# One level of Strassen's scheme for the gate and up products of a two-layer hybrid block, on one core of a Trainium2 chip

## The reference

```
def swiglu(x, w_gate, w_up, w_down):
    return (jax.nn.silu(x @ w_gate) * (x @ w_up)) @ w_down
x = x + 0.5 * swiglu(rms_norm(x, norm), w_gate, w_up, w_down)   # D_MODEL = 1024, D_FF = 2816
```

## Time and profile before

| | us |
|---|---|
| three runs, median (lowest to highest) | 1998.88 (1998.53 to 1999.64) |
| span of the profiled execution, first to last instruction | 1996.9 |
| TensorE busy | 1968.5 |
| VectorE busy | 1076.8 |
| ScalarE busy | 771.1 |
| GpSimd busy | 50.0 |

### The profile page before, as it was taken

How to read it: one execution, slowest core, us unless ns; L and a number is a source line. 1 busy time by engine, 2 the same in 40 slices (tenths; PEclk the granted TensorE clock), 3 DMA queues, 4 the chain that set the end, 5 groups by cost and what they waited for, 6 DMA issues and landing times.

```text
span 1996.9 us, 25404 instructions
## 1 busy us (share of the span) xinstructions
PE 1968.5 (99%) x9054; PEld 1613.8 (81%) x9054; DVE 1076.8 (54%) x1673; ACT 771.1 (39%) x1110; POOL 50.0 (3%) x86
## 2 busy tenths in 40 slices
PE   7999999999999999999999999999999999999999
PEld 5888888888778888888888888877778778888887
DVE  5444444767674444446544444456989854444444
ACT  4222222477773222224332222354555852223222
POOL 1000000000000000000000000011111000000000
PEclk9999999999999999999999999999999999999999
DMA  4254433321122222233322233267765352332223
GB/s 166 101 122 121 137 96 100 110 74 64 55 84 95 95 95 96 99 100 105 106 95 95 95 96 102 96 163 168 158 153 133 87 137 96 97 103 95 95 95 105
DMA packets 60863, 213.80 MB, mean 107 GB/s; under 512 B 6616, under 2 KB 6872, under 8 KB 60792
## 3 DMA queue, kind: packets, MB, share of 16 engines
q1 hardware_dynamic: 52080, 184.97, 28.2%
q0 software_dynamic: 6192, 22.55, 6.2%
q10 hardware_dynamic: 2520, 5.36, 1.5%
HBM read 185.32 MB, written 4.72 MB: 95 GB/s over the span
## 4 chain that ended last, share of the span: by engine, by line
PE 89%; DVE 6%; ACT 3%; issue 2%; DMA 0%; SPq 0%; DVEq 0%; ACTq 0%
PE ps_unit L546 28%; PE ps_unit L548 28%; PE ps_unit L547 28%; DVE cv L1795 1%; DVE isc L1776 1%; PE ps_t L675 1%; DVE top L1774 1%; PE ps_s L546 1%; PE ps_y L547 0%; PE ps_y L548 0%; ACT w_hi L947 0%; PE ps_y L546 0%; PE ps_misc L636 0%; ACT L962 0%; DVE pt_lo L1543 0%
## 5 line engine op out<-in xcount | busy, mean ns | idle before, releaser
L947 ACT ACTIVATE w_hi<-raw 128x1024 fp32r<-128x1024 f32 x301 | 319.2, 1061 | 1019.9 <-PE ps_unit L548 1009.8
L546 PE MATMUL ps_unit<-xs_hi,w_hi 128*128 128x512 f32 x1768 | 697.3, 394 | 11.9 <-DVE xs_lo L1358 11.1
L547 PE MATMUL ps_unit<-xs_lo,w_hi 128*128 128x512 f32 x1768 | 688.9, 390 | 0.0
L548 PE MATMUL ps_unit<-xs_hi,w_lo 128*128 128x512 f32 x1696 | 660.9, 390 | 0.0
L1350 DVE TENSOR_TENSOR w_lo<-raw,w_hi 128x1024 fp32r<-128x1024 f32 x301 | 368.1, 1223 | 84.4 <-ACT w_hi L947 84.3
L546 PEld LDWEIGHTS ps_unit<-xs_hi,w_hi 128*128 128x128 f32 x1768 | 332.3, 188 | 87.8 <-DVE w_lo L1350 9.3
L547 PEld LDWEIGHTS ps_unit<-xs_lo,w_hi 128*128 128x128 f32 x1768 | 332.6, 188 | 68.5 <-issue 1.7
L548 PEld LDWEIGHTS ps_unit<-xs_hi,w_lo 128*128 128x128 f32 x1696 | 318.8, 188 | 66.9
L546 PE MATMUL ps_unit<-a_hi,w_hi 128*128 128x512 f32 x892 | 350.4, 393 | 2.4 <-DVE t L1472 0.8
L547 PE MATMUL ps_unit<-a_lo,w_hi 128*128 128x512 f32 x892 | 347.5, 390 | 0.0
L548 PE MATMUL ps_unit<-a_hi,w_lo 128*128 128x512 f32 x845 | 329.2, 390 | 0.0
(11 more groups left out here) (236 smaller groups left out, 1292.6 us busy)
## 6 DMA issues: line engine op xcount, KB each, us to landing
raw<-w_stream_dram SPq DMA_DIRECT2D x344, 512.0 KB, 3.5
w_lo<-raw POOLq DMA_DIRECT2D x28, 512.0 KB, 5.2
w_lo_3rd<-raw POOLq DMA_DIRECT2D x15, 512.0 KB, 5.3
skew<-table ACTq DMA_DIRECT2D x1, 2560.0 KB
bias_t<-skew ACTq DMA_DIRECT2D x1, 2048.0 KB, 9.7
out_dram<-xt SPq DMA_DIRECT2D x8, 256.0 KB, 2.0
xt<-xt_in_dram SPq DMA_DIRECT2D x7, 256.0 KB, 6.0
bd_raw<-bd_in_dram SPq DMA_DIRECT2D x1, 512.0 KB, 8.1
```

The source lines that it names most:

```text
L546: pe.matmul(ps, lhs_hi, rhs_hi, start=first, stop=False)
L547: pe.matmul(ps, lhs_hi, rhs_lo, start=False, stop=False)
L548: return pe.matmul(ps, lhs_lo, rhs_hi, start=False, stop=last)
L947: act.activation(w_hi[:, s, :], raw[:, slot, :], ACT.Copy).then_inc(w_hi_done, 1)
```

## The change

Gate and up of a hidden tile form one product: the weights' two column halves (gate, up) by the two token halves, with channels taken in pairs of blocks. One level of Strassen's scheme (in Winograd's form) gives it by seven products of half-size blocks. Each product is 4 block pairs x 3 matmuls of 256 columns, so 84 matmuls where there were 48 of 512 columns.

- **Weights.** Gate and up weights come in a stream of their own, `gu_stream`, two transfers of 512 KB a tile, into two slots of `gu` (4 pieces of 128x512 each). GpSimd makes four sums of pieces a tile (`sums`), each over 128x512. ACT and DVE split seven pieces a tile (`gw_high`, `gw_low`: three operations of 128x1024, one of 128x512), one tile ahead.
- **Activations.** DVE and ACT build four operands for each pair of x tiles besides the plain halves (`even_x`, `odd_x`, with their `_lo` and `_hi`), in place of `split_x` ahead of an FFN stage. The squares of an FFN stage are summed on GpSimd (`squares_added`).
- **Products.** Their results are combined in PSUM and in SBUF: some accumulate onto each other in banks of `ps_s` and `ps_t`; a chain of three runs in `ps_y`, and ACT copies it out after each step (`chain_copy`). DVE's subtractions give gate and up.
- **Order.** Down products, their units and groups stay. FFN stages are written out instead of looped. SP issues the loads of tiles and units in one written order. Constants for attention and one transfer move behind the first FFN.

The core of the diff (semaphore declarations, buffer addresses and the start-up left out):

```
...
+            def gu_load(f):
+
+                if f >= 2 and f not in after_mixer:
+                    sp.wait_ge(gw_lo_done, split_count(f - 2, 3))
+                for part in range(2):
+                    sp.dma_start(gu[:, 4 * (f % 2) + 2 * part:4 * (f % 2) + 2 * part + 2, :],
+                                 gu_stream[f, part]).then_inc(gu_landed[f % 2], 16)
...
+            def sums(f):
+
+                r = f % 2
+                a11, a21, a12, a22 = (gu[:, 4 * r + k, :] for k in range(4))
+                s1, s2, s4 = (gu[:, k, :] for k in (8, 9, 10))
+                pool.wait_ge(gu_landed[r], 32 * (f // 2 + 1))
+                if f:
+                    pool.wait_ge(gw_lo_done, split_count(f - 1, 0))
+                nc.gpsimd.tensor_tensor(s1, a21, a22, ALU.add).then_inc(sum_done, 1)
+                if f:
+                    pool.wait_ge(gw_lo_done, split_count(f - 1, 1))
+                pool.wait_ge(sum_done, 4 * f + 1)
+                nc.gpsimd.tensor_tensor(s2, s1, a11, ALU.add).then_inc(sum_done, 1)
+                if f:
+                    pool.wait_ge(gw_lo_done, split_count(f - 1, 2))
+                pool.wait_ge(sum_done, 4 * f + 2)
+                nc.gpsimd.tensor_tensor(s4, s2, a12, ALU.add).then_inc(sum_done, 1)
+                nc.gpsimd.tensor_tensor(a21, a21, a11, ALU.add).then_inc(sum_done, 1)
...
+            def gu_product(ps, piece, hi, lo, first, wait=None):
+
+                for j in range(PAIRS):
+                    if wait:
+                        wait(j)
+                    w = slice(j * P, (j + 1) * P)
+                    pe.matmul(ps, gw_hi[:, piece, w], hi(j), start=first and j == 0, stop=False, skip_group_check=True)
+                    pe.matmul(ps, gw_hi[:, piece, w], lo(j), start=False, stop=False, skip_group_check=True)
+                    mm = pe.matmul(ps, gw_lo[:, piece, w], hi(j), start=False, stop=j == PAIRS - 1, skip_group_check=True)
+                mm.then_inc(prod_done, 1)
...
+                pe.wait_ge(gw_lo_done, split_count(f, 0))
+                if f >= 2:
+                    pe.wait_ge(gate_done, f - 1)
+                gu_product(bank(r, 0, 1), 1, *of_u(0, 1), True, landed(ua_done))
+                if f:
+                    pe.wait_ge(copy_done, 4 * f)
+                gu_product(chain, 0, *of_u(0, 0), True)
+                pe.wait_ge(gw_lo_done, split_count(f, 1))
+                pe.wait_ge(copy_done, 4 * f + 1)
+                gu_product(bank(r, 0, 0), 2, *of_u(1, 0), False, landed(ub_done))
+                pe.wait_ge(copy_done, 4 * f + 2)
+                gu_product(chain, 3, *of_xu(1), False, landed(uc_done))
...
+                pe.wait_ge(gw_lo_done, split_count(f, 2))
+                gu_product(bank(r, 0, 1), 5, *of_u(1, 1), False)
+                pe.wait_ge(copy_done, 4 * f + 3)
+                gu_product(chain, 4, *of_xu(0), False)
...
+                pe.wait_ge(gw_lo_done, split_count(f, 3))
+                if f >= 2:
+                    pe.wait_ge(up_done, f - 1)
+                gu_product(bank(r, 1, 0), 6, *of_xu(2), True)
...
+            def gw_high(f, k):
+
+                w, src = gu_split(k, f % 2)
+                act.wait_ge(sum_done, 4 * f + (1, 2, 4, 4)[k])
+                if f:
+                    act.wait_ge(prod_done, 7 * (f - 1) + (2, 4, 6, 7)[k])
+                act.activation(gw_hi[:, w, :], src, ACT.Copy).then_inc(gw_hi_done, 1)
...
+                act.activation(bank(r, 1, 1), bank(r, 0, 1), ACT.Copy).then_inc(copy_done, 1)
+                if j:
+                    hidden_hi(f - 1, j - 1)
+                if f:
+                    act.wait_ge(gate_done, f)
...
+                chain_copy(f, 2, sqb[:, 0, 0:TH])
+                if more:
+                    gw_high(f + 1, 0)
+                chain_copy(f, 4, sqb[:, 0, TH:T])
+                if i is not None:
+                    norm_std(i)
+                if more:
+                    gw_high(f + 1, 1)
+                if f:
+                    act.wait_ge(up_done, f)
+                chain_copy(f, 6, sqb[:, 1, 0:TH])
+                act.wait_ge(gate_scaled, f + 1)
...
                 act.activation(t1[:, :], t0[:, :], ACT.Silu).then_inc(silu_done, 1)
...
+                if more:
+                    gw_high(f + 1, 2)
+                    gw_high(f + 1, 3)
...
+            def gw_low(f, k):
+
+                w, src = gu_split(k, f % 2)
+                dve.wait_ge(gw_hi_done, split_count(f, k))
+                dve.tensor_tensor(gw_lo[:, w, :], src, gw_hi[:, w, :].bitcast(F32), ALU.subtract).then_inc(gw_lo_done, 1)
+
+            def hidden(f, j, more, i=None):
+
+                r = f % 2
+                if more:
+                    gw_low(f + 1, 0)
+                if i is not None:
+                    norm_diag(i)
+                dve.wait_ge(prod_done, 7 * f + 5)
+                dve.wait_ge(copy_done, 4 * f + 3)
+                if f:
+                    dve.wait_ge(silu_done, f)
+                dve.tensor_tensor(t0[:, :], sqb[:, 0, :], bank(r, 0), ALU.subtract).then_inc(gate_done, 1)
+                if i is not None:
+                    norm_rstd(i)
+                dve.wait_ge(gate_done, f + 1)
+                dve.tensor_tensor(t0[:, :], t0[:, :], rstd[:, :], ALU.mult).then_inc(gate_scaled, 1)
+                if more:
+                    gw_low(f + 1, 1)
+                dve.wait_ge(prod_done, 7 * f + 7)
+                dve.wait_ge(copy_done, 4 * f + 4)
+                twice = sqb[:, 1, 0:TH].rearrange("p (o t) -> p o t", o=1).to_broadcast([P, 2, TH])
+                dve.tensor_tensor(t2[:, :].rearrange("p (h t) -> p h t", t=TH), twice,
+                                  bank(r, 1).rearrange("p (h t) -> p h t", t=TH), ALU.subtract).then_inc(up_done, 1)
+                dve.wait_ge(up_done, f + 1)
+                dve.wait_ge(silu_done, f + 1)
+                dve.tensor_tensor(t2[:, :], t2[:, :], t1[:, :], ALU.mult).then_inc(hidden_done, 1)
+                if more:
+                    gw_low(f + 1, 2)
+                dve.wait_ge(a_hi_done, f + 1)
+                dve.tensor_tensor(a_lo[:, j * T:(j + 1) * T], t2[:, :], a_hi[:, j * T:(j + 1) * T].bitcast(F32),
+                                  ALU.subtract).then_inc(a_lo_done, 1)
+                if more:
+                    gw_low(f + 1, 3)
...
+            def odd_x(i, j):
+
+                s, x, g, n = scr_even(i, j), xt_tile(2 * j + 1), gain("norm", i * KT + 2 * j + 1), PAIRS * FFN_NO[i] + j + 1
+                if n > 1:
+                    dve.wait_ge(uc_done, n - 1)
+                dve.scalar_tensor_tensor(scr[:, 3, :], x[:, TH:T], g, s[:, 2, :], ALU.mult, ALU.subtract).then_inc(u76_done, 1)
+                dve.wait_ge(u76_done, 2 * n - 1)
+                dve.scalar_tensor_tensor(scr[:, 4, :], scr[:, 3, :], -1.0, s[:, 0, :], ALU.mult, ALU.subtract).then_inc(u76_done, 1)
+                dve.wait_ge(u76_done, 2 * n)
+                dve.scalar_tensor_tensor(scr[:, 5, :], x[:, 0:TH], g, scr[:, 4, :], ALU.mult, ALU.add).then_inc(u4_done, 1)
...
+                            dve.wait_ge(x_added, X_BASE[i] + g * KT + d + 1)
+                            next_x(i + 1, d)
```

More of the change, by code:

```diff
@@ L403, in gain, with minus, pieces, gu_split @@
             return vec[:, ds(COL[col] + d, 1)]
+        def minus(d):
+            return minus_gain[:, ds(d, 1)]
+        def pieces(a, b):
+            return gu[:, a:b + 1:b - a, :]
+        def gu_split(k, r):
+            src = (pieces(4 * r, 8), pieces(4 * r + 2, 9), pieces(4 * r + 1, 10), gu[:, 4 * r + 3:4 * r + 4, :])[k]
+            return slice(2 * k, min(2 * k + 2, 7)), src
+        def split_count(f, k):
+            return 4 * f + k + 2
+        chain = ps_y[:, 0:TH]
+        def bank(r, which, part=None):
+            b = (ps_s, ps_t)[which][:, r, :]
+            return b if part is None else b[:, part * TH:(part + 1) * TH]
+        def scr_even(i, j):
+            return scr_first[:, j, :, :] if i == 0 else scr[:, 0:3, :]
         @block.sync
@@ L540, in _, with ffn @@
                     add_raw(n)
+            def ffn(i):
+                f0 = FFN_BASE[i]
+                behind_ffn = i > 0 and PHASES[i - 1] == "ffn"
+                if not behind_ffn:
+                    sums(f0)
+                squares_added(i)
+                if i == 0:
+                    sums(1)
+                    softplus()
+                further = 2 if i + 1 < len(PHASES) and PHASES[i + 1] == "ffn" else 0
+                for f in range(f0 + (2 if behind_ffn or i == 0 else 1), FFN_BASE[i + 1] + further):
+                    sums(f)
+            for i, phase in enumerate(PHASES):
+                {"ffn": ffn, "even": even, "odd": odd}[phase](i)
         @block.tensor
@@ L983, in ffn @@
             def ffn(i):
-                n0, tile0 = UNIT_BASE[i], FFN_BASE[i]
-                pair(n0, 0, tile0, n0, norm=i)
-                n, tile = n0, tile0
+                n, tile = UNIT_BASE[i], FFN_BASE[i]
```

(8 more changed lines are left out.)

505 lines of the change are left out of this document (316 added, 189 removed).

## The result

The change made the kernel slower: 2106.41 us median of 4 runs (2104.17 to 2110.8), 1.0543 times before (95% interval 1.0528 to 1.0558). The forecast was 2067 us, range 1955 to 2115. The profiled execution took 2107.26 us, its span is 2104.7 us.

What follows compares the result with a forecast made beforehand. TensorE, 99% busy, was taken to bound the kernel before; DVE and GpSimd blocking each other would slow the changed tiles. +29 + 7 + 18 + 8 + 6 = +68 us on 1998.9 gave 2067 us, range 1955 to 2115.

Steps and rivals of the forecast that it cites:

- TensorE's part: Hidden tiles: 84 narrow matmuls 0.12 us apart take 10.08 us instead of 10.87, saving 70 us over 88 tiles.
- The port, both ways: Hidden tiles: GpSimd additions and DVE operations with two SBUF inputs exclude each other, whichever comes second waiting fully.
- The tile under contention: Hidden tiles with DVE and GpSimd blocking each other: 11.5 us, between 10.7 and 12.3; +29 us over four FFNs.
- The transitions: Start, entries into FFN stages and their first tiles: extra work delays TensorE, +7, +18, +8 and +6 us.
- (a): FFN 2 into FFN 3: DVE's longer x tile work and blocking by the squares cost +7 us (2 to 16).
- (b): Mixer into FFN, twice: an already full DVE gets some 12 us more; +9 each, 18 us (6 to 40).
- (c): Start: even tiles, two weight halves and one sum come before TensorE's first product; +8 us (3 to 18).
- (d): Each FFN's first tile: two table loads ahead of copies in ACT's queue; +1.5 x 4 = 6 us (0 to 12).
- Rival 1: Hidden tiles: GpSimd is held back only at its start, TensorE keeps the bound, faster; 1960 us, chance 0.18.
- Rival 2: Hidden tiles at the floor: only GpSimd waits, or it fills DVE's PSUM reads and idle times; 2003 us, chance 0.13.
- Rival 4: Hidden tiles: narrow matmuls don't hold 0.12 us; at 0.135 a tile is 11.3 us; 2071 us, chance 0.05.
- rival 3: Tiles all serial, +93 us, and long transitions, 60 us; 2150 us, chance 0.11.

Runs made afterwards that it cites:

- run 9: Against the changed kernel with weight sums and squares moved from GpSimd to DVE (2034.28 us): the four sums placed later in DVE's order, behind the hidden tile's product; 1983.49 us.
- run 1: Changed kernel with GpSimd's weight sums cut to 4 of 512 columns, except for tiles 0, 1, 22 and 66; 1989.26 us.
- run 2: Changed kernel with GpSimd's additions of the squares cut to 4 of 512 columns, the first copy of each phase whole; 2085.69 us.
- run 3: Changed kernel with both GpSimd's weight sums and its additions of the squares cut to 4 of 512 columns, one execution; 1969.49 us.
- run 8: Against a kernel with sums on DVE and DMA, FFN squares on TensorE (2062.23 us): at the start, ACT's first copy and two down splits reordered; 2060.27 us.
- 11: Against late sums with A21 + A11 by DMA (1989.58 us): down splits moved into first tiles, last weight splits behind x, start's copy earlier; 1988.43 us.
- 12: Against run 9: at the three later FFN entries, down splits moved into the first tile; behind mixers, last two weight splits behind the last x tile; 1980.07 us.

## Why the prediction was right, and where it was off

- **TensorE's part: right.** The weight loads (LDWEIGHTS) inside a product stand 0.11 to 0.12 us apart, in the changed kernel and then in run 9 (timelines of PEld):

```profile
91.31 0.19 PEld L756 LDWEIGHTS ps_s<-xs_lo,gw_hi 128*128 128x128 f32 x1
91.42 0.19 PEld L757 LDWEIGHTS ps_s<-xs_hi,gw_lo 128*128 128x128 f32 x1
91.54 0.19 PEld L755 LDWEIGHTS ps_s<-xs_hi,gw_hi 128*128 128x128 f32 x1
```

```profile
91.40 0.19 PEld L715 LDWEIGHTS ps_y<-xs_hi,gw_hi 128*128 128x128 f32 x1
91.51 0.19 PEld L716 LDWEIGHTS ps_y<-xs_lo,gw_hi 128*128 128x128 f32 x1
91.63 0.19 PEld L717 LDWEIGHTS ps_y<-xs_hi,gw_lo 128*128 128x128 f32 x1
```

  Where nothing held it back, the tile was 9.76 us, 0.1162 per matmul, against 10.08: a term of -98 instead of -70 us. The 109 ns by the formula of the Trainium skill (TensorE: Matmul & The Clock Gate, Back-to-back issue gap), which the section gives as the gap of an isolated matmul, were not reached. The runs lie between them and the 0.12 us of the earlier trace rows, nearer to the rows.
- **DVE's own tile of 7.5 us: right.** In run 1, one tile (length, busy us and count of PE, PEld, DVE, ACT, POOL; clock; DMA):

```profile
82.00:91.76 9.76, 9.76 (x87) 9.76 (x86) 7.46 (x9) 5.93 (x11) 1.94 (x4) 1.00 0.34 117
```

  With four sums more, run 9's DVE is busy 9.69 us of a tile of 9.76.
- **GpSimd's addition: right**, 1.29 us on average for the 12 sums that met no DVE operation, against 1.2. Beside DVE, 1.8 to 2.4 us were forecast; the average over all 352 is 1.59.
- **The port, both ways: right**, the step on which the sign rested and which no row of before could show. DVE's side of it is the 1.219 against 2.305 us above, and the sums' removal was worth 117 us. The Trainium skill (SBUF — State Buffer, Who interferes with whom) states this lock for both; the trace of the changed kernel agrees, with 140 splits and 256 sums that waited for the other.
- **The tile under contention: slightly high**, 11.5 forecast, 11.25 measured. Hidden parts and the rest came to +16.4 us against +29 + 6. The forecast let TensorE run ahead through a group and stall 8.8 us at its end for the last a_lo. In the trace it is held back in every tile instead, and all its waits at the down products for a_lo sum to 22.0 us, none above 3.5.
- **The transitions: the step that was mis-sized.** (a), (b), (c) were +7, +18, +8 = 33 us and measured 17.5, 47.2 and 26.7 = 91.4 (with a part of (d)'s 6 in them): each lies above its upper bound of 16, 40 and 18. What was missing is known in part. The blocking by the squares, which (a) names without a price of its own, came to 19 us in all (run 2), and the sums of tile 1 beside the last odd x tile cost some 4 us more (run 3). "4 us of cover, since TensorE needs only even tiles first" didn't exist in use: the third product needs ACT's copy, which stands behind all x tiles in ACT's order (42.18 above; run 8 took 6.6 us off the first norm by moving it). And TensorE, left idle, came back at half rate: about 137 of the narrow matmuls around the entries stood 0.21 us apart instead of 0.117, some 13 us of TensorE's time. How much of that reached the span isn't shown: 22 of them stand ahead of the 17 us of idle time at the start, where they cost nothing. With all but 16 of GpSimd's sums cut, and the squares, 65 us remain (run 3). How they divide between DVE's amount, the odd tile's chain of five operations and ACT's order stays open: the order runs 8, 11 and 12 moved only 0 to 7 us of an entry.
- **Rival 1, GpSimd in the way only at its start: excluded** by runs 1 to 3. Its price for tiles without contention was good in the sum (1960 against 1969 in run 3), by two errors that cancel: entries 34 us worse, everything else 25 us better. Rival 2 took it that only GpSimd waits, which the 140 delayed splits exclude, or that GpSimd's work hides in full behind DVE's other work: the tile came 0.5 us above that floor of 10.7. Rival 4 is excluded by matmuls 0.117 us apart, and rival 3 by the tile of 11.25, though its transitions of 60 us were the nearest forecast of those measured.
- The sum was 39 us too low, 58 from the entries against 19 that tiles and first tiles were too high. The range held the time by 9 us, and that is luck in part: with the 19 us at their forecast the time would have been 2125, above its end at 2115. The sign and the cause were not luck.

## What to carry to other kernels

An engine that looks free is free only for work that doesn't meet the busy engine's operands: before moving SBUF-to-SBUF work to GpSimd, add its time to that of DVE's operations with two SBUF inputs. If the sum (here 4.8 + 5.9 = 10.7 us) exceeds the tile that TensorE could reach (9.76), and DVE has room for the work, keep it on DVE; here that alone took 63 us off. Then look for an instruction that waits for a load in front of work that the bound engine needs: moving four additions down DVE's queue, nothing else, was worth another 51 us. And price each entry into a pipelined stage as a stage of its own, with every queue's order in it and TensorE's rate after an idle time.

## What the runs showed of the hardware

- The spacing of its matmuls shows at which of its two clocks TensorE comes back from idle time. The first 24, behind 20.0 us of it, stood 0.21 us apart from the second to the last:

```profile
20.40 0.41 PE L756 MATMUL ps_s<-xs_lo,gw_hi 128*128 128x256 f32 x1
20.61 0.42 PE L757 MATMUL ps_s<-xs_hi,gw_lo 128*128 128x256 f32 x1
```

  At the later entries the granted clock shows the same. Behind 4.0 us of idle time, the matmuls from 1037.4 us on stood 0.21 us apart at a granted clock of 0.50, which is the level of 1.2 GHz; from 1043.7 us on they stood 0.11 to 0.12 us apart at 1.00, 2.4 GHz. TensorE's row in the view by stretch (length, busy us, clock, DMA):

```profile
1038.00:1041.80 3.80, 3.80 (x20) 0.50 0.02 4
1044.00:1046.00 2.00, 2.00 (x19) 1.00 0.00 0
```

  The clock of 1.00 in the stretch 20 to 24 us above is no reading: the clock records of this trace begin at 26.0 us, and the view prints 1.00 where it has none. The kernel before started so too: where nothing held them, its 512-wide matmuls stood 0.43 us apart until 14.6 us and 0.23 us from 14.9 us on, where its clock records begin.
- A short operation pays the same wait at the port as a long one. Of the 88 narrow splits, 0.684 us alone, 82 began while a sum ran and took 1.781 us on average. So the narrow split (1.706 us mean) costs almost what the wide one does (1.797).
- Two blocked engines both look busy. GpSimd's sums rose from 1.29 to 1.59 us on average, and DVE's busy share of 80% on the page holds some 295 us that vanish in run 1 (1693 to 1398 us).
